# Norm statistics with tokens on partitions in a two-layer diffusion trunk

## The chip, the cores and the metric

The kernel is one program on one NeuronCore of a Trainium2 chip. The metric is the device time of one execution in microseconds (us). The engines are named as the profile names them: PE is TensorE's matmul, PEld its load of the stationary operand, DVE is VectorE, ACT is ScalarE, POOL is GpSimd, and SP issues the DMAs. They run side by side and meet at semaphores.

## The reference, cut to what matters

The trunk has two layers over 256 context tokens and 256 latent tokens, each with 1024 channels. A layer is a half-step SwiGLU, a token mixing of four head groups, and a second half-step SwiGLU. Every branch is normalised before it (with a modulation) and after it (with a gate):

```python
def rms_norm(x, g):
    y = xf * lax.rsqrt(jnp.mean(xf * xf, axis=-1, keepdims=True) + RMS_EPS)
    return y * g
def modulate(x, g_pre, shift, scale):
    return rms_norm(x, g_pre) * (1.0 + scale) + shift
def half_ffn(v, shift, scale, gate, g_pre, g_post, w1, w3, w2):
    out = swiglu(modulate(v, g_pre, shift, scale), w1, w3, w2)
    return v + 0.5 * gate * rms_norm(out, g_post)
```

These norms run over the 1024 channels of a token, so each needs one number per token: the reciprocal root of the mean of squares. There are twelve of them, six per layer. In the last layer the context tokens are dropped after the mixing, so three of the twelve cover the 256 latent tokens only.

## The kernel before, in words

The activations lie transposed in SBUF: channels on the 128 partitions, in `KC` = 8 blocks `m`, and the `T` = 512 tokens along the free dimension (four tiles of 128 tokens; tiles 0 and 1 are context, 2 and 3 latent). A sum over channels is thus a sum over partitions, done on PE, and the result has to be spread back over all partitions.

One norm has four steps. (1) `token_sums` (line 806): for each block of squares and each tile of 128 tokens one matmul with 32 columns of ones as the stationary operand and the 128 columns of squares as the moving one. Tile `i` writes partitions `32*i` to `32*i+31` of a PSUM bank, columns 0 to 127. (2) ACT `norm` (line 1535): a root over that [128 x 128] region into `root`. (3) DVE `norm` (line 2073): its reciprocal into `inverse`. (4) `spread` (line 796): one matmul per tile, a column of the constants that picks the tile's row (broadcast to 128 columns) as the stationary operand and `inverse` as the moving one, which puts the tile's 128 reciprocals on every partition of bank columns `128*i` and on. DVE then multiplies by the bank.

The twelve norms sit in these places. The first is at the start (`start_sums`, line 813; squares by DVE in `setup_x`), behind the products of the first modulation pieces. Ten more make five pairs, each pair in a gap between two long stages of weight products: `postnorm` (line 833) closes a branch, and `prenorm` (line 819) opens the next. The twelfth closes the last layer. In `postnorm` DVE has already added up seven of the eight blocks of squares into `yacc`, so that PE sums two blocks: `yacc` and the last one. Then DVE scales the eight blocks (line 2132) and adds them to `xT` (line 2136; two of the adds on POOL, line 2728). In `prenorm` ACT squares each block as soon as it is added (line 1573), and PE sums all eight blocks one after the other, in the order in which they come.

Each gap also has three products of the modulation (`mod_product`, line 786, 16 matmul records each), written into PE's order by hand: the first ahead of the postnorm's sums, the second behind the prenorm's sums of block `m == 2`, the third between the last sums and the `spread`. PE executes in program order. After the spread, DVE and ACT work through the eight blocks (DVE line 2100, ACT lines 1593 and 1599, DVE line 2109), and PE takes each block for the first weight piece of the next stage as it comes. The weights are split in two parts of lower precision by ACT (line 1533) and DVE (line 2024), and a weight product is three matmuls (lines 853 to 855). The DMAs of the weights wait for slots of a ring and not for the norms.

Of the kernel before, what the change touches and what calls it, by code (L numbers as in the profile page):

```python
# [20 lines left out]
ACT = mybir.ActivationFunctionType  # L21
AX = mybir.AxisListType.X

P = 128
# [12 lines left out]
C_TILE = C_SEL + 32  # L37
# [50 lines left out]
def trunk(nc, out, consts, x, c, ctx, c_ctx, w_mod, b_mod, norm_g, ffn1_w1, ffn1_w3, ffn1_w2,  # L88
# [3 lines left out]
    LAYERS, D, _ = w_in.shape  # L92
# [10 lines left out]
    NT = T // P  # L103
# [64 lines left out]
    MOD_GROUPS, at = [], 0  # L168
# [21 lines left out]
    with es:  # L190
        ARENA = 30336

        def sb(name, shape):
            return es.enter_context(nc.sbuf_tensor(name, shape, F32))
# [7 lines left out]
        cst = sb("cst", [P, C_END])  # L202
# [11 lines left out]
        epsc = sb("epsc", [P, 2])  # L214
# [10 lines left out]
        def sem(name):  # L225
            if name not in sems:
                sems[name] = es.enter_context(nc.semaphore(name))
            return sems[name]

        ident = cst[:, C_IDENT:C_IDENT + P]  # L230
        ones = cst[:, C_ONES:C_ONES + P]
# [5 lines left out]
        def view(at, *shape, parts=slice(0, P)):  # L237
            n = int(np.prod(shape))
            v = arena[parts, at:at + n]
            if len(shape) == 1:  # L240
                return v
            names = "abcd"[:len(shape)]
            return v.rearrange(f"p ({' '.join(names)}) -> p {' '.join(names)}",
                               **{k: s for k, s in zip(names, shape)})
# [14 lines left out]
        silu_t = view(27648, 2, T)  # L259
        sq_in, u_in = view(8192, KC, T), view(0, KC, T)  # L260
        ul_spare = view(7680, T)
        root, inverse = view(28160, P), view(28288, P)
        yacc = view(28672, T)

        convT = view(0, 12, T)
# [125 lines left out]
        inverse_ready, inverse_spread = sem("inverse_ready"), sem("inverse_spread")  # L391
# [9 lines left out]
        sums_ready, rms_ready = sem("sums_ready"), sem("rms_ready")  # L401
# [100 lines left out]
        def tiles_of(hs):  # L502
            return [2 * h + i for h in hs for i in range(2)]
# [22 lines left out]
        def quadrants(hs):  # L526
            return slice(64 * hs[0], P)
# [209 lines left out]
        def _(pe):  # L737
# [58 lines left out]
            def spread(n, bank, hs):  # L796

                pe.wait_ge(inverse_ready, n + 1)
                at = quadrants(hs)
                for i in tiles_of(hs):  # L800
                    last = pe.matmul(bank[:, i * P:(i + 1) * P],  # L801
                                     cst[at, C_TILE + i:C_TILE + i + 1].to_broadcast([P - at.start, P]),
                                     inverse[at, :], start=True, stop=True)
                last.then_inc(inverse_spread, 1)

            def token_sums(bank, squares, hs, first, last):

                for i in tiles_of(hs):
                    done = pe.matmul(bank[32 * i:32 * i + 32, 0:P], ones[:, 0:32], squares[:, i * P:(i + 1) * P],
                                     start=first, stop=last)  # L810
                return done

            def start_sums():
                for m in range(KC):
                    pe.wait_ge(x_squared, m + 1)
                    done = token_sums(ps[PRE_BANK], squares_of(0)[:, m, :], (0, 1), m == 0, m == KC - 1)
                done.then_inc(sums_ready, 1)

            def prenorm(l, j, second=None, third=None):
                hs = pre_halves(l, j)  # L820
                for m in range(KC):
                    pe.wait_ge(x_squared, 8 * (3 * l + j) + m + 1)
                    done = token_sums(ps[PRE_BANK], squares_of(j)[:, m, :], hs, m == 0, m == KC - 1)
                    if m == 2 and second is not None:
                        mod_product(second, ps[GAP_BANK])
                done.then_inc(sums_ready, 1)
                if third is not None:
                    mod_product(third, ps[GAP_BANK])
                spread(6 * l + 2 * j, ps[PRE_BANK], hs)
                if third is not None:  # L830
                    mod_turn(third, ps[GAP_BANK])

            def postnorm(l, j, first):
                hs = post_halves(l, j)
                q = 3 * l + j
                if first is not None:
                    mod_product(first, ps[GAP_BANK])
                pe.wait_ge(y_summed, (KC - 2) * (q + 1))
                token_sums(ps[POST_BANK], yacc, hs, True, False)
                pe.wait_ge(y_sq, KC * (q + 1))  # L840
                token_sums(ps[POST_BANK], ysq_of(j), hs, False, True).then_inc(sums_ready, 1)
                spread(6 * l + 2 * j + 1, ps[POST_BANK], hs)
# [615 lines left out]
            pe.wait_ge(sem("mod_params_in"), 16 * MOD_PARAM_DMAS)  # L1458
            setup_params(0, ps[2])
            spread(0, ps[PRE_BANK], (0, 1))  # L1460
            mod_group(2, ps[6])
            pe.wait_ge(mod_copied, 4)
# [19 lines left out]
        def _(act):  # L1482
            meet = meeting(act)
            link = linked(act, sem("act_link"))
            A = nc.scalar.activation
# [48 lines left out]

            def norm(n, bank, hs):
                act.wait_ge(sums_ready, n + 1)
                at = quadrants(hs)
                A(root[at, :], bank[at, 0:P], ACT.Sqrt, bias=epsc[at, 0:1], scale=1.0 / D).then_inc(rms_ready, 1)

            def gain(l, j, m, hs):  # L1540

# [24 lines left out]
            def prenorm(l, j, third=None):  # L1566

                hs = pre_halves(l, j)
                t0 = HALF * hs[0]
                p = 3 * l + j  # L1570
                for m in range(KC):
                    wait_x(act, p - 1, m)
                    A(squares_of(j)[:, m, t0:T], xT[:, m, t0:T], ACT.Square).then_inc(x_squared, 1)
                norm(6 * l + 2 * j, ps[PRE_BANK], hs)
                if third is not None:
                    mod_row_out(third, ps[GAP_BANK])
                prenorm_blocks(l, j, third)
# [25 lines left out]
            def gap(l, j):  # L1603
                third = gap_mods(l, j)[-1]
                hs = post_halves(l, j)
                norm(6 * l + 2 * j + 1, ps[POST_BANK], hs)
                for m in range(KC - 2, KC):
                    gain(l, j, m, hs)
                if after(l, j)[0] < LAYERS:
                    prenorm(*after(l, j), third)  # L1610
# [356 lines left out]
            mod_group(0, ps[0])  # L1967
            round_piece(PIECES["up0", 0, 0][0], 2048)
            norm(0, ps[PRE_BANK], (0, 1))
            setup_mod_params()  # L1970
            mod_group(2, ps[6])
# [19 lines left out]
        def _(dve):  # L1991
            meet = meeting(dve)
            link = linked(dve, sem("dve_link"))
            V = nc.vector
# [77 lines left out]

            def norm(n, hs):
                dve.wait_ge(rms_ready, n + 1)
                at = quadrants(hs)
                V.reciprocal(inverse[at, :], root[at, :]).then_inc(inverse_ready, 1)  # L2076

            def split_in(l, j):
                split_rest(PIECES["in", l][j], KC * IN_WIDTH[j], (wh_in, wl_in))
# [1 line left out]
            def prenorm(l, j):  # L2081
                hs = pre_halves(l, j)
                n = 6 * l + 2 * j
                pre_gains(l, j)
                norm(n, hs)
                prenorm_blocks(l, j)
# [36 lines left out]
            def postnorm(l, j, hs):  # L2123
                t0 = HALF * hs[0]
                q, n = 3 * l + j, 6 * l + 2 * j + 1
                norm(n, hs)
                dve.wait_ge(inverse_spread, n + 1)
                for m in range(KC + 1):
                    if m < KC:
                        y = uT[:, m, t0:T]  # L2130
                        dve.wait_ge(y_gained, KC * q + m + 1)
                        TT(y, y, ps[POST_BANK][:, t0:T], ALU.mult).then_inc(y_scaled, 1)  # L2132
                    if m and m - 1 not in POOL_ADDS:
                        dve.wait_ge(y_scaled, KC * q + m)
                        x = xT[:, m - 1, t0:T]
                        TT(x, x, uT[:, m - 1, t0:T], ALU.add).then_inc(x_ready, 1)  # L2136
# [539 lines left out]
            setup()  # L2676
            setup_x()
            norm(0, (0, 1))
            split_rest(PIECES["up0", 0, 0][0], 2048)
            dve.wait_ge(sem("params_act"), 1)  # L2680
# [231 lines left out]
```

## Time and profile before

| | us |
|---|---|
| median of 3 runs | 2231.27 |
| lowest and highest | 2228.21 and 2235.86 |
| the profiled execution, its own time | 2232.0 |
| span of the profiled execution | 2230.2 |
| PE busy in the span | 2080.8 (93%) |
| DVE, ACT, POOL busy | 1080.7, 795.0, 186.3 |

The span runs from the first to the last instruction, and 1.8 us of the execution's own time lie outside it. An fp32 matmul stands in the trace as two records, each with its own load record (PEld). A record's duration includes its way through the pipeline, so that neighbours overlap: what a stream of them costs is the distance from start to start. The column of the granted clock is a share of full speed: 1.00 is 2.4 GHz, 0.50 is 1.2 GHz.

### The profile page before, as it was taken

The numbers are of one execution on the slowest core, as the hardware profiler recorded it, in microseconds if no ns is written. First come the engines' busy times: TensorE is split into PE (matmuls) and PEld (weight loads), VectorE is DVE, ScalarE is ACT, GpSimd is POOL, SyncE is SP. The second block draws the span as 40 slices with busy tenths as digits, with TensorE's granted clock in tenths as the row PEclk, the third lists the DMA queues.
The fourth block names the chain that finished last, engine by engine and source line by source line (L and its number), as shares of the span: only waits on it lengthen the run. The fifth ranks groups of instructions, "written<-read, shape, count | busy, mean of one in ns | idle before, by whom it ended". The sixth has DMA issues, their size and how long they took to land.

```text
span 2230.2 us, 30926 instructions
## 1 busy us (share of the span) xinstructions
PE 2080.8 (93%) x13065; PEld 1711.7 (77%) x13065; DVE 1080.7 (48%) x1604; ACT 795.0 (36%) x1203; POOL 186.3 (8%) x288
## 2 busy tenths in 40 slices
PE   6999999899989998999999899999979987879997
PEld 4778888687846876888888688888858865678997
DVE  5233334566285586333334533333475557575555
ACT  4232223454336335222223522222253434245343
POOL 0000000100024321000000100000010023420000
PEclk9999999899999999999999999999988998999999
DMA  9563442422236424324323432432332311345662
GB/s 303 158 176 115 132 115 84 134 83 93 73 116 221 145 90 111 97 72 127 95 71 111 130 89 78 126 95 66 115 115 70 110 35 58 114 133 161 178 165 84
DMA packets 403322, 258.92 MB, mean 116 GB/s; under 512 B 21850, under 2 KB 402032, under 8 KB 403184
## 3 DMA queue, kind: packets, MB, share of 16 engines
q1 hardware_dynamic: 403184, 256.94, 39.3%
q8 instruction: 103, 1.69, 0.3%
q14 instruction: 35, 0.29, 0.0%
HBM read 255.86 MB, written 1.05 MB: 115 GB/s over the span
## 4 chain that ended last, share of the span: by engine, by line
PE 81%; DVE 12%; ACT 3%; issue 2%; SPq 1%; POOL 1%; DMA 0%; DVEq 0%; ACTq 0%; POOLq 0%
PE bank L853 23%; PE bank L855 23%; PE bank L854 23%; PE bank L786 2%; DVE uT L2132 1%; PE bank L1220 1%; DVE mlaw L2358 1%; DVE arena L2365 1%; DVE xT L2136 1%; DVE small L2386 1%; PE bank L1358 1%; DVE wl L2024 1%; PE bank L801 1%; ACT wh L1533 0%; DVE arena L2076 0%
## 5 line engine op out<-in xcount | busy, mean ns | idle before, releaser
L853 PE MATMUL bank<-uh,wh 128*128 128x512 f32 (+1 forms) x1504 | 548.7, 365 | 14.5 <-DVE ul L2109 6.7
L854 PE MATMUL bank<-ul,wh 128*128 128x512 f32 (+1 forms) x1504 | 546.0, 363 | 0.0
L855 PE MATMUL bank<-uh,wl 128*128 128x512 f32 (+1 forms) x1504 | 545.8, 363 | 0.0
L2024 DVE TENSOR_TENSOR wl<-ring,wh 128x2048 fp32r<-128x2048 f32 (+1 forms) x155 | 312.4, 2016 | 156.2 <-ACT wh L1533 155.3
L1533 ACT ACTIVATE wh<-ring 128x2048 fp32r<-128x2048 f32 (+1 forms) x158 | 267.1, 1691 | 310.5 <-PE bank L855 293.2
L853 PEld LDWEIGHTS bank<-uh,wh 128*128 128x128 f32 x1504 | 286.5, 190 | 64.7 <-issue 12.2
L855 PEld LDWEIGHTS bank<-uh,wl 128*128 128x128 f32 x1504 | 286.2, 190 | 43.9
L854 PEld LDWEIGHTS bank<-ul,wh 128*128 128x128 f32 x1504 | 286.6, 191 | 42.8
L853 PE MATMUL bank<-hh,wh 128*128 128x512 f32 (+1 forms) x704 | 255.5, 363 | 1.4 <-DVE wl L2024 1.4
L855 PE MATMUL bank<-hh,wl 128*128 128x512 f32 (+1 forms) x704 | 255.2, 362 | 0.0
L854 PE MATMUL bank<-hl,wh 128*128 128x512 f32 (+1 forms) x704 | 255.2, 362 | 0.0
L2154 DVE TENSOR_TENSOR arena<-arena,bank 128x512 f32<-128x512 f32 (+1 forms) x88 | 54.6, 621 | 370.8 <-PE bank L855 370.8
L1629 ACT ACTIVATE hh<-arena 128x512 fp32r<-128x512 f32 (+1 forms) x88 | 50.9, 579 | 412.3 <-DVE arena L2154 412.3
L853 PEld LDWEIGHTS bank<-hh,wh 128*128 128x128 f32 x704 | 132.9, 189 | 22.3 <-DVE wl L2024 1.7
L855 PEld LDWEIGHTS bank<-hh,wl 128*128 128x128 f32 x704 | 132.9, 189 | 20.7
L854 PEld LDWEIGHTS bank<-hl,wh 128*128 128x128 f32 x704 | 132.9, 189 | 20.5
L853 PE MATMUL bank<-uTh,wh_in 128*128 128x512 f32 (+2 forms) x320 | 126.3, 395 | 13.0 <-DVE ul_in L2109 7.4
L855 PE MATMUL bank<-uTh,wl_in 128*128 128x512 f32 (+2 forms) x320 | 122.6, 383 | 0.0
L854 PE MATMUL bank<-ul_in,wh_in 128*128 128x512 f32 (+2 forms) x320 | 122.5, 383 | 0.0
L1627 ACT ACTIVATE arena<-bank 128x512 f32<-128x512 f32 (+1 forms) x88 | 47.9, 544 | 160.9 <-PE bank L855 160.9
L1686 ACT ACTIVATE arena<-bank 128x512 f32<-128x512 f32 (+5 forms) x64 | 30.5, 479 | 177.1 <-PE bank L855 176.8
L853 PEld LDWEIGHTS bank<-uTh,wh_in 128*128 128x128 f32 (+1 forms) x320 | 63.7, 199 | 31.5 <-issue 8.5
(322 smaller groups left out, 2660.6 us busy)
## 6 DMA issues: line engine op xcount, KB each, us to landing
ring<-in_ffn_w_dram SPq DMA_DIRECT2D x176, 512.0 KB, 5.2
ring<-in_w_mod_dram SPq DMA_DIRECT2D x134, 512.0 KB, 4.5
ring<-in_ffn_w_dram SPq DMA_DIRECT2D x64, 384.0 KB, 3.4
ring<-in_ffn_w_dram SPq DMA_DIRECT2D x64, 320.0 KB, 4.1
ring<-in_w_in_dram SPq DMA_DIRECT2D x40, 512.0 KB, 4.5
ring<-in_w_out_dram SPq DMA_DIRECT2D x16, 512.0 KB, 4.5
arena<-in_w_mod_dram SPq DMA_DIRECT2D x10, 512.0 KB, 8.6
ring<-in_w_in_dram SPq DMA_DIRECT2D x4, 544.0 KB, 5.4
```

The lines of the kernel that those rows point to most:

```text
L786: product = pe.matmul(bank[at, 256:512], scT[:, own:own + 32], weights[:, k * 256:(k + 1) * 256], start=g == first and k < 4, stop=g == fi ...
L801: last = pe.matmul(bank[:, i * P:(i + 1) * P], cst[at, C_TILE + i:C_TILE + i + 1].to_broadcast([P - at.start, P]), inverse[at, :], start=T ...
L853: pe.matmul(bank, w_hi, x_hi, start=first, stop=False)
L854: pe.matmul(bank, w_hi, x_lo, start=False, stop=False)
L855: return pe.matmul(bank, w_lo, x_hi, start=False, stop=last)
L1220: last = pe.matmul(bank[:, h * P:(h + 1) * P], gates[:, 5, t, c0:c0 + 1].to_broadcast([P, P]), tri(d), start=False, stop=h == NH - 1, skip ...
L1533: A(high[:, SPLIT[n] % 2, 0:floats], ring[:, n % RING, 0:floats], ACT.Copy).then_inc(wh_ready, 1)
L1627: A(silu_t[:, j % 2, t0:T], ps[2 * (j % 2)][:, t0:T], ACT.Silu).then_inc(silu_done, 1)
L1629: A(hh[:, j, t0:T], silu_t[:, j % 2, t0:T], ACT.Copy).then_inc(hh_ready, 1)
L1686: A(dst, src, ACT.Copy, scale=scale).then_inc(proj_copied, 1)
L2024: TT(low[:, b, 0:floats], at, high[:, b, 0:floats].bitcast(F32), ALU.subtract).then_inc(wl_ready, 1)
L2154: TT(ht, ht, ps[2 * (j % 2) + 1][:, t0:T], ALU.mult).then_inc(gated, 1)
```

## The change

The sums turn round. Each [128 x 128] tile of squares becomes the stationary operand, loaded in full, and a single column of ones the moving one. Tile `i`'s sums land in column `i` of the bank, one token per partition. The root and the reciprocal then work on [128 x 4] in place of [128 x 128] (on [128 x 2] where only the latent tokens count, in place of [64 x 128]). The spread takes a column of `inverse`, broadcast to 128 columns, as the stationary operand and the identity as the moving one. The number of matmuls does not change in any step, and neither do the order of the work or the semaphores.

```diff
-        root, inverse = view(28160, P), view(28288, P)
+        root, inverse = view(28160, NT), view(28288, NT)
...
                 pe.wait_ge(inverse_ready, n + 1)
-                at = quadrants(hs)
                 for i in tiles_of(hs):
-                    last = pe.matmul(bank[:, i * P:(i + 1) * P],
-                                     cst[at, C_TILE + i:C_TILE + i + 1].to_broadcast([P - at.start, P]),
-                                     inverse[at, :], start=True, stop=True)
+                    last = pe.matmul(bank[:, i * P:(i + 1) * P], inverse[:, i:i + 1].to_broadcast([P, P]), ident,
+                                     start=True, stop=True)
...
             def token_sums(bank, squares, hs, first, last):
                 for i in tiles_of(hs):
-                    done = pe.matmul(bank[32 * i:32 * i + 32, 0:P], ones[:, 0:32], squares[:, i * P:(i + 1) * P],
-                                     start=first, stop=last)
+                    done = pe.matmul(bank[:, i:i + 1], squares[:, i * P:(i + 1) * P], ones[:, 0:1],
+                                     start=first and i == tiles_of(hs)[0], stop=last, skip_group_check=True)
...
                 act.wait_ge(sums_ready, n + 1)
-                at = quadrants(hs)
-                A(root[at, :], bank[at, 0:P], ACT.Sqrt, bias=epsc[at, 0:1], scale=1.0 / D).then_inc(rms_ready, 1)
+                at = slice(2 * hs[0], NT)
+                A(root[:, at], bank[:, at], ACT.Sqrt, bias=epsc[:, 0:1], scale=1.0 / D).then_inc(rms_ready, 1)
...
                 dve.wait_ge(rms_ready, n + 1)
-                at = quadrants(hs)
-                V.reciprocal(inverse[at, :], root[at, :]).then_inc(inverse_ready, 1)
+                at = slice(2 * hs[0], NT)
+                V.reciprocal(inverse[:, at], root[:, at]).then_inc(inverse_ready, 1)
```

## Rows read from the trace of the kernel before

**Rows 1.** The page: busy time by engine, then the chain of waits by line.
```profile
PE 2080.8 (93%) x13065; PEld 1711.7 (77%) x13065; DVE 1080.7 (48%) x1604; ACT 795.0 (36%) x1203; POOL 186.3 (8%) x288
...
PE bank L853 23%; PE bank L855 23%; PE bank L854 23%; PE bank L786 2%; DVE uT L2132 1%; PE bank L1220 1%; DVE mlaw L2358 1%; DVE arena L2365 1%; DVE xT L2136 1%; DVE small L2386 1%; PE bank L1358 1%; DVE wl L2024 1%; PE bank L801 1%; ACT wh L1533 0%; DVE arena L2076 0%
```

**Rows 2.** Chain of waits, first gap: start us, us, what.
```profile
419.03 0.47 PE bank L809 x8
...
419.52 0.38 ACT arena L1538
...
419.92 0.96 DVE arena L2076
...
431.92 0.47 PE bank L809 x8
...
433.82 1.17 PE bank L801 x8
...
449.96 2.30 DVE wl_in L2024
```

**Rows 3.** Timeline, first gap: start us, us, instructions [idle before].
```profile
418.34 0.40 PE L809 MATMUL bank<-arena,cst 128*32 128x128 f32 x8
...
426.98 1.29 ACT L1573 ACTIVATE arena<-xT 128x512 f32<-128x512 f32 x2 [0.51 <-POOL xT L2728]
...
427.66 0.65 PE L809 MATMUL bank<-arena,cst 128*32 128x128 f32 x8 [0.48 <-ACT arena L1573]
...
428.09 1.93 PE L786 MATMUL bank<-ring,scT 128*32 128x256 f32 x16
...
429.79 1.29 PE L809 MATMUL bank<-arena,cst 128*32 128x128 f32 x24
...
432.16 1.05 PE L786 MATMUL bank<-ring,scT 128*32 128x256 f32 x16
```

**Rows 4.** Timeline of PE and PEld, full loads with few moving columns.
```profile
1764.19 1.98 PEld L1002 LDWEIGHTS bank<-gates,cst 128*128 128x128 f32 x16
...
1766.09 0.97 PEld L1005 LDWEIGHTS bank<-gates,cst 128*128 128x128 f32 x8
...
1766.12 1.04 PE L1005 MATMUL bank<-gates,cst 128*128 128x16 f32 x8
...
562.94 0.53 PEld L1005 LDWEIGHTS bank<-gates,cst 128*128 128x128 f32 x3
...
563.05 0.42 PEld L1005 LDWEIGHTS bank<-gates,cst 128*128 128x128 f32 x2
```

**Rows 5.** Lines L1939 (a root) and L2394 (a reciprocal): ns min/median/max.
```profile
L1939 ACT ACTIVATE std<-small,epsc x3: 281/281/283, 795.5 to 1971.1; 128x4 f32<-128x4 f32 x3
...
L2394 DVE RECIPROCAL small<-small x24: 138/156/167, 642.3 to 1878.6; 128x2 f32<-128x2 f32 x24
```

**Rows 6.** Windows: length, busy us (records) by engine, granted clock, DMA share, GB/s.
```profile
428.00:430.00 2.00, 2.00 (x28) 1.06 (x24) 2.00 (x5) 0.93 (x3) 1.66 (x1) 0.50 1.07 346
430.00:432.00 2.00, 1.47 (x39) 0.66 (x32) 1.54 (x5) 1.83 (x3) 0.00 (x0) 0.99 1.07 326
...
560.70:562.40 1.70, 1.70 (x17) 1.69 (x16) 0.00 (x0) 1.47 (x3) 0.00 (x0) 1.00 0.00 0
562.40:563.40 1.00, 1.00 (x10) 1.00 (x10) 0.00 (x0) 1.00 (x3) 0.00 (x0) 0.89 0.00 0
563.40:565.00 1.60, 1.60 (x5) 1.31 (x6) 0.77 (x5) 1.60 (x2) 0.00 (x0) 0.50 0.00 0
```

**Rows 7.** Timeline of PE, the start.
```profile
19.31 1.52 PE L809 MATMUL bank<-arena,cst 128*32 128x128 f32 x48
...
24.40 2.08 PE L801 MATMUL bank<-arena,cst 128*128 128x128 f32 x8 [1.61 <-DVE arena L2076]
```

**Rows 8.** Timeline of ACT, the start.
```profile
23.01 0.35 ACT L1538 ACTIVATE arena<-bank,epsc 128x128 f32<-128x128 f32 x1
...
34.69 0.38 ACT L1507 ACTIVATE mod_row<-bank 128x256 f32<-128x256 f32 x1 [0.38 <-PE bank L786]
```

**Rows 9.** Timeline, fifth gap, latent tokens only.
```profile
2007.72 1.71 PE L809 MATMUL bank<-arena,cst 128*32 128x128 f32 x14
...
2010.11 0.36 ACT L1538 ACTIVATE arena<-bank,epsc 64x128 f32<-64x128 f32 x1 [2.17 <-PE bank L809]
...
2011.51 0.71 PE L801 MATMUL bank<-arena,cst 64*128 64x128 f32 x4 [0.34 <-DVE arena L2076]
```

**Rows 10.** Chain of waits, the last norm.
```profile
2213.97 0.44 PE bank L809 x4
...
2214.43 0.37 ACT arena L1538
2214.83 0.96 DVE arena L2076
```

## The prediction

> **What bounds the kernel now.** I read the page first. PE is busy 93% of the span, and the chain that ended last runs through the three lines of weight products for 69% [rows 1]. The root (L1538), the reciprocal (L2076) and the spread (L801) stand in it with about 1% or less each. So the change can touch only the start, the five gaps and the last norm. The chain through the first gap comes next [rows 2]: the sums of the last block, root, reciprocal and spread follow each other with nothing beside them, in the postnorm (419.03 to 422.1) and in the prenorm (431.92 to 435.0). The chain then runs through DVE and ACT to the split of the next weights at 449.96. What the spread gains or loses, the end of the gap gains or loses. The timeline of the same gap [rows 3] shows how PE's own queue stands around that chain, and this decides the case. Four of the five gaps have all 512 tokens and look alike to within 0.1 us; the fifth and the last norm have 256.
>
> **The price of a sum.** Before, eight records (four tiles, two records each) cost little, because the load has 32 columns and the four tiles write four groups of partitions: 24 records, three blocks, take 1.29 us [rows 3], 0.05 us from start to start. Afterwards each record loads 128 columns. The nearest rows are the gate sums, full fp32 loads with 8 or 16 moving columns: sixteen loads in 1.98 us, then eight in 0.97 [rows 4]; less the 0.19 of one load, that is 0.11 us from start to start. At half clock the starts are 562.94 and 563.05 [rows 4], again 0.11. No row has a single moving column; 8 and 16 columns give the same, so I take 0.11 at either clock. A block of four tiles then costs 0.88 us on PE. The ends for one record are 0.05 (this kernel's 32-column records) and 0.13 (full loads with 128 columns in the spread: 1.17 us for eight, less the tail, at full clock).
>
> **Root and reciprocal.** The root now takes 0.37 us on [128 x 128]; a root on [128 x 4] takes 0.28 [rows 5]. The reciprocal takes 0.95; on [128 x 2] it takes 0.16 [rows 5]. Together they save 0.9 us a norm, bounded by 0.8 and 1.0.
>
> **Spread.** It has the same number of records, the same 128 loaded and 128 moving columns, and a broadcast stationary operand as before: nothing, at the same clock. With 256 tokens it now contracts over 128 rows and not 64; I take nothing there too, bounded by 0.1 either way.
>
> **Postnorm, 512 tokens (four).** The last sums stand in the chain with 0.47 us [rows 2]; eight full loads take 1.04 [rows 4], so +0.6. The sums of `yacc` start at 418.34 [rows 3] and ran beside DVE's square, which ends just before 419.03. At 0.11 us a record they now end about 0.1 later than that, so +0.1. With the 0.9 saved, each postnorm gains 0.2 us.
>
> **Prenorm, 512 tokens (four).** Here PE has a queue. Square 2 is ready at 427.6, its sums run at 427.66, the second product runs from 428.09 to 429.79, a start-to-start time of 1.70 us at half clock, and then three waiting blocks are caught up in 1.3 us, so that the last block is summed 0.5 us after its square, at 432.4 [rows 2, 3]. Afterwards, all moved 0.2 earlier by the postnorm: sums of block 2 end at 427.4 + 0.9 = 428.3; the product ends at 430.0; blocks 3 to 7 are forty records, 4.4 us, and end at 434.4. The squares no longer matter, they come every 0.6 us and a block costs 0.88. That is 2 us late. The root and the reciprocal follow (0.2 of PE's tail, 0.28, 0.16, the hops): ready at 435.1. But the third product stands ahead of the spread in PE's order. Before, it ran at 432.16 for 1.05 us [rows 3] under the root and the reciprocal, which were longer. Now it starts at 434.4 and ends at 435.4 at full clock, or at 436.1 if it takes 1.70 as the second one does at half clock. So the short root and reciprocal are worth nothing beyond this product, and the spread starts at 435.4 to 436.1 where it started at 433.82 [rows 2]: +1.6 to +2.3, the postnorm's gain already in it.
>
> **The clock.** Under the second product the granted clock was 0.50 (1.2 GHz), and it rose behind it, so that the third product and the spread ran at 2.4 GHz [rows 6]. Under the gate sums, full loads with 8 and 16 moving columns, PE was busy all the time; the clock was 1.00 in their first part, 0.89 in the second, and 0.50 behind them, though PE had not been idle [rows 6]. The new sums are such work, with one column. So 4.4 us of them between the second product and the spread can leave the spread at 1.2 GHz. There it costs 2.08 us [rows 7] and not 1.17: +0.9 a gap. I take about half of this: one full gap costs 1.6 (warm throughout) to 3.2 us (cold throughout), taken at 2.4. Four make +9.6, bounded by 6.4 and 12.8. The Trainium skill, "TensorE: Matmul & The Clock Gate" (Part 1), says that the gate follows how busy PE has been; by that rule alone the new sums would hold the clock up, and the sum would be the warm one. The row of the gate sums disagrees.
>
> **Start.** The sums start at 19.31 behind the modulation products [rows 7]; 64 records at 0.11 take 7 us and end at 26.3. The root started at 23.01 [rows 8]: +3.3, less 0.9, so the spread starts 2.4 later than 24.40, and it ran at half clock already [rows 7]. Behind it PE's modulation products and ACT's blocks move by as much. At 34.69 ACT had waited 0.38 us for a product behind a DMA [rows 8]; this absorbs a part, a clock that rises earlier another. I take +1.8, bounded by 1.2 and 2.4.
>
> **256 tokens.** The fifth gap's sums run at half clock, 14 records in 1.71 us, already 0.1 a record [rows 9], so they do not grow. The root waits for PE as before at 2010.11, and the third product now ends beside the old start of the spread at 2011.51: −0.3. Its postnorm and the last norm have four records: 0.44 [rows 10] becomes about 0.65, and 0.9 goes: −0.7 each. Together −1.7, bounded by −2.2 and −1.
>
> **Sum.** 9.6 + 1.8 − 1.7 = +9.7 us on the profiled execution's own 2232.0 us: 2241.7. That execution lies 0.7 us above the median of the runs; against the median I predict 2241 us, 0.4% slower. All parts at their warm ends give 6.4 + 1.2 − 2.2 = +5.4, at their cold ends 12.8 + 2.4 − 1.0 = +14.2, so the forecast's own range is 2237 to 2246. What a measurement of this kernel tells from no change is 0.3%, 6.7 us.
>
> **Rivals.**
>
> *The loads turn out cheap (faster).* If a full load hides behind its predecessor, a record costs what the old ones cost. Then root and reciprocal pay: −1.0 in each postnorm; in each prenorm the third product ends at 433.2 and lets the spread start 0.6 earlier. Four gaps give −6.4, the fifth and the last −2.4, the start nothing, since ACT's root there waited for ACT itself: 2222. It decides below 0.07 us a record: 428.3 + 1.7 + 40 records + 1.0 then meets 433.82. For it: weight products with 512 columns hide their loads. Against it: 0.11 us in 24 rows of the gate sums [rows 4]. The same page (back-to-back issue gap) gives about 60 cycles for a matmul with 1 to 64 columns, 25 ns, when the load is left out; by that rule this rival would be the forecast.
>
> *Warm and absorbed (no change).* The clock stays at 2.4 GHz in the gaps, the second product too (0.7 us less in each), and the start is absorbed: 4 × 1.0 + 1 − 1.7 = +3.3, 2234 to 2238. For it: the clock rises in the gap today, with sums among the work (0.99 in the stretch behind the second product) [rows 6]. Against it: before that product DVE and ACT leave PE idle in every gap, and the clock is at 0.50 there now [rows 6].
>
> *The cold clock reaches into the next stage (slower still).* If it also delays the weight products behind the spread by more than PE's idle time at the end of the gap (the wait for the split at 449.96 [rows 2]), each gap costs 2 us more: +20, 2248 to 2253. Against it: these products follow DVE's and ACT's pace.
>
> **Chances.** Forecast 0.52, no change 0.25, cold beyond 0.13, faster 0.10. The forecast's lowest part lies within 0.3%. This makes faster 0.10, same 0.31, slower 0.59. The range takes in the no-change case from 2233 up and the cold one to 2251.
>
> **What would show it.** After: PEld records of L809's line with 128 columns, 0.11 us apart; a root near 0.28 and a reciprocal near 0.16; in the four full gaps the last prenorm sums end 2 us later behind an unbroken row of loads, the third product directly behind, the spread directly behind that, not behind the reciprocal; the spread at 2.1 us in some gaps; the last norm 0.7 shorter. Records 0.06 apart, or PE waiting for squares again, would make it wrong.

## The result, and the profile after

| | before | after |
|---|---|---|
| median, us | 2229.95 (4 runs, 2228.21 to 2235.86) | 2278.98 (4 runs, 2276.77 to 2283.06) |
| ratio to before | 1 | 1.0205, 95% interval [1.0174, 1.0236] |
| the profiled execution: own time, span, mean granted clock | 2232.0, 2230.2, 0.968 | 2283.06, 2281.3, 0.947 |

The change makes the kernel 2% slower, 49 us, where 10 us were predicted. The profiled execution after is the longest of its four and lies 4 us above their median. The clock has two levels, so a mean of 0.947 over 2281.3 us means 2 × 0.053 × 2281.3 = 242 us at half clock; before it was 2 × 0.032 × 2230.2 = 143 us.

The page of the kernel after: busy time by engine, the granted clock in 40 slices, the chain by line, and the groups of the sums' line.

```profile
PE 2152.7 (94%) x13065; PEld 1789.0 (78%) x13065; DVE 1072.1 (47%) x1604; ACT 794.1 (35%) x1203; POOL 186.2 (8%) x288
...
PEclk8999999799999997999999799999979998898998
...
PE bank L851 23%; PE bank L853 22%; PE bank L852 22%; PE bank L807 4%; PE bank L786 3%; PE bank L1218 1%; PE bank L800 1%; DVE mlaw L2356 1%; PE bank L1356 1%; DVE arena L2363 1%; PE bank L1121 1%; DVE wl L2022 1%; ACT uT L1591 1%; DVE small L2384 1%; PE bank L1327 0%
...
L807 PEld LDWEIGHTS bank<-cst,arena 128*128 128x128 f32 x432 | 82.9, 297 | 22.4 <-ACT arena L1571 17.7
L807 PE MATMUL bank<-cst,arena 128*128 128x1 f32 x432 | 84.4, 328 | 14.9 <-ACT arena L1571 13.3
```

PE is busier than before (94% against 93% of a longer span) and does no more products: as many records, 13065, as in [rows 1]. The sums (L807 now, L809 before) have entered the chain with 4%, some 90 us; the reciprocal has left its list. The first gap shows how. Chain of waits of the kernel after: start us, us, what.

```profile
424.14 1.89 PE bank L807 x16
426.06 0.27 ACT arena L1536
...
426.59 1.17 PE bank L800 x8
...
430.26 0.64 ACT arena L1571
430.95 5.28 PE bank L807 x24
436.23 1.86 PE bank L786 x16
438.09 8.62 PE bank L807 x40
446.71 1.86 PE bank L786 x16
448.57 2.02 PE bank L800 x8
...
463.57 1.91 ACT wh_in L1531
465.56 2.30 DVE wl_in L2022
```

From 430.95 to 450.6 everything is PE. Before, the chain went through squares, root and reciprocal here [rows 2, 3]. The forty records after the second product take 8.62 us, 0.215 each. The sixteen of the postnorm take 1.89, 0.118 each with the tail of the last one; their load records alone take 1.86 us, which less the 0.19 of one load is 0.11 from start to start. The same instruction has two prices, and the windows of the kernel after say what goes with them (length, busy us of PE, PEld, DVE, ACT and POOL with their records, granted clock, DMA share, GB/s):

```profile
424.00:426.00 2.00, 2.00 (x20) 1.86 (x16) 0.60 (x1) 1.09 (x1) 0.83 (x1) 1.00 0.00 0
427.00:431.00 4.00, 0.80 (x8) 0.61 (x6) 3.22 (x5) 1.55 (x4) 2.77 (x2) 0.66 0.07 7
431.00:435.00 4.00, 4.00 (x19) 4.00 (x20) 4.00 (x8) 2.43 (x4) 2.65 (x2) 0.50 1.01 328
...
438.02:446.64 8.62, 8.62 (x44) 8.61 (x41) 0.00 (x0) 0.00 (x0) 0.00 (x0) 0.50 0.42 129
...
451.00:458.00 7.00, 4.70 (x13) 3.67 (x13) 6.39 (x12) 6.30 (x13) 0.00 (x0) 0.50 0.40 116
458.00:463.00 5.00, 5.00 (x22) 4.08 (x21) 4.25 (x8) 4.53 (x8) 0.00 (x0) 0.90 0.00 0
```

PE is idle between the postnorm's spread and the first square of the prenorm, and the clock falls there (a mean of 0.66 from 427 to 431). In the kernel before it was at 0.50 under the second product, too, and up again behind it [rows 6]. Now it stays at 0.50 through 8.62 us in which PE is busy without a gap, through the third product and the spread, and on into the weight products until about 458.

The line of the sums, of the root and of the reciprocal (ns min/median/max) in the kernel after:

```profile
L807 PEld LDWEIGHTS bank<-cst,arena x432: 186/333/338, 19.1 to 2266.1; 128*128 128x128 f32 x144
...
L1536 ACT ACTIVATE arena<-bank,epsc x12: 262/263/264, 30.4 to 2266.4; 128x4 f32<-128x4 f32 x9, 128x2 f32<-128x2 f32 x3
...
L2074 DVE RECIPROCAL arena<-arena x12: 165/178/179, 30.6 to 2266.7; 128x4 f32<-128x4 f32 x9, 128x2 f32<-128x2 f32 x3
```

The root (0.26) and the reciprocal (0.18) are as short as they were priced. A load is 186 ns at its shortest and 333 in the median, so more than half of the 432 loads ran at the low clock.

Where the 51.1 us of span went. Each row is a stretch of the two traces. A gap is taken here from the start of the postnorm's spread to the start of the split of the next weights on DVE (L2024 before, L2022 after).

| stretch | before | after | difference |
|---|---|---|---|
| start to the first postnorm's spread | 420.9 | 426.6 | +5.7 |
| four full gaps | 29.0, 28.4, 28.4, 29.0 | 39.0, 39.1, 38.2, 38.6 | +40.0 |
| from each to the next postnorm's spread | 407.0, 354.2, 354.2, 350.8 | 409.9, 354.2, 354.3, 350.6 | +2.8 |
| fifth gap | 20.2 | 24.8 | +4.6 |
| from there to the end | 208.0 | 206.0 | −2.0 |

So the loss is in the gaps and at the start. Behind the spread nothing is added but the spread's own length: in the first gap it ends at 434.99 before and at 450.59 after, and the split follows 14.97 us behind both; the other three are alike. The weight products at half clock until 458 are not on the chain. In the long stages the two kernels are level, but for 2.9 us in the first layer's token mixing. No experiment separates these; e10 below, with the same start and prenorms, does not have them.

### The profile page after: what moved, and what is told of

The parts are those of the page before. It is cut to its first block, busy times and chain, and to the rows that moved or that the text cites. A ratio compares the mean times of both kernels' runs of the same rounds, so it can differ in the third digit from the quotient of the medians.

```text
span 2281.3 us, 30926 instructions
## 1 busy us (share of the span) xinstructions
PE 2152.7 (94%) x13065; PEld 1789.0 (78%) x13065; DVE 1072.1 (47%) x1604; ACT 794.1 (35%) x1203; POOL 186.2 (8%) x288
## 4 chain that ended last, share of the span: by engine, by line
PE 84%; DVE 10%; ACT 3%; issue 1%; POOL 1%; DMA 0%; DVEq 0%; SPq 0%; ACTq 0%; POOLq 0%
PE bank L851 23%; PE bank L853 22%; PE bank L852 22%; PE bank L807 4%; PE bank L786 3%; PE bank L1218 1%; PE bank L800 1%; DVE mlaw L2356 1%; PE bank L1356 1%; DVE arena L2363 1%; PE bank L1121 1%; DVE wl L2022 1%; ACT uT L1591 1%; DVE small L2384 1%; PE bank L1327 0%
## 5 line engine op out<-in xcount | busy, mean ns | idle before, releaser
L2022 DVE TENSOR_TENSOR wl<-ring,wh 128x2048 fp32r<-128x2048 f32 (+1 forms) x155 | 312.5, 2016 | 152.1 <-ACT wh L1531 151.3
L807 PEld LDWEIGHTS bank<-cst,arena 128*128 128x128 f32 x432 | 82.9, 297 | 22.4 <-ACT arena L1571 17.7
L807 PE MATMUL bank<-cst,arena 128*128 128x1 f32 x432 | 84.4, 328 | 14.9 <-ACT arena L1571 13.3
```

Of the source, the lines that this page charges most:

```text
L807: done = pe.matmul(bank[:, i:i + 1], squares[:, i * P:(i + 1) * P], ones[:, 0:1], start=first and i == tiles_of(hs)[0], stop=last, skip_gr ...
L2022: TT(low[:, b, 0:floats], at, high[:, b, 0:floats].bitcast(F32), ALU.subtract).then_inc(wl_ready, 1)
```

## The experiments

The theory for all of them: the sums lose by what they do on PE, in the prenorms and at the start, and half of the loss is the clock. Such loads with one moving column cost 0.11 us at 2.4 GHz and 0.215 at 1.2 GHz, and they do not bring the clock back. The rival: something in the order of the work (third product ahead of the spread, short root and reciprocal with nothing to hide) costs it, and the clock is a bystander.

**e1: 128 moving columns.** The ones become 128 columns, and the root reads one column of each tile; all else is as in the kernel after.

```diff
-                    done = pe.matmul(bank[:, i:i + 1], squares[:, i * P:(i + 1) * P], ones[:, 0:1],
+                    done = pe.matmul(bank[:, i * P:(i + 1) * P], squares[:, i * P:(i + 1) * P], ones,
```

> The changed kernel, but each full load of squares is followed by 128 moving columns of ones and not by one (the same sums in 128 columns, the root reads one of them). Same number of loads and records. Theory A (one moving column leaves PE's clock at 1.2 GHz behind the first idle stretch of a gap, and a full load takes twice as long there): 128 moving columns let the clock rise in the gap, the time at half clock falls from 244 us to 150-190, and the kernel takes 2240-2258 us, faster than the changed one (2279) although it does more. Theory B (PE's time for full loads alone, the clock follows how long PE is busy): no gain, 2279-2290 us, time at half clock still about 240.

Measured: 2246.18 us, ratio 1.0052 [1.0036, 1.0067]. Three quarters of the loss (2.05% in the kernel after, 0.52% here) is gone by adding work. The time at half clock is 126 us, less than the 150 to 190 expected. Chain and then windows of this kernel, first gap:

```profile
424.78 5.49 PE bank L807 x24
430.27 1.20 PE bank L786 x16
431.46 4.66 PE bank L807 x40
436.13 1.00 PE bank L786 x16
437.13 1.10 PE bank L800 x8
```

```profile
424.78:430.20 5.42, 5.42 (x25) 5.20 (x25) 5.42 (x10) 3.26 (x6) 3.28 (x2) 0.50 1.03 334
430.20:431.40 1.20, 1.20 (x18) 0.46 (x17) 0.80 (x4) 1.12 (x2) 0.00 (x0) 0.81 0.77 237
431.40:436.10 4.70, 4.70 (x48) 4.58 (x47) 0.00 (x0) 0.00 (x0) 0.00 (x0) 1.00 0.75 232
```

At 0.50 a record takes 0.229 us, hardly more than with one column; then the clock rises during the second product, and the forty records take 0.117 each. So the moving columns hardly change the pace at either clock, and the price of a load doubles, nearly, when the clock halves. With one moving column the clock did not come back here, with 128 it did.

In the third gap of this kernel the clock is never down. Windows, and the postnorm's spread and the split of the next weights from the chain:

```profile
1248.00:1255.80 7.80, 5.12 (x47) 3.90 (x46) 6.99 (x12) 4.09 (x8) 3.08 (x2) 1.00 0.57 144
1255.80:1262.00 6.20, 6.20 (x64) 5.45 (x61) 2.02 (x7) 2.48 (x5) 0.25 (x1) 1.00 0.62 169
```

```profile
1247.62 1.17 PE bank L800 x8
...
1277.58 2.30 DVE wl L2022
```

From spread to split it is 30.0 us, where this gap takes 28.4 before and 38.2 after. So with every load at full clock the queue on PE costs 1.6 us in this gap, and the other 8.2 of the change's 9.8 go with the low clock. The other three full gaps of e1, whose first 24 loads run at half clock as above, cost 3.6 to 4.0 us. These and the start make up what is left, 0.52% or some 12 us.

**e2: the long root and reciprocal back.** On top of the former, ACT and DVE work on 128 columns again (and the spread picks its columns of `inverse` accordingly).

```diff
-                A(root[:, at], bank.rearrange("p (i n) -> p i n", n=P)[:, at, 0], ACT.Sqrt, bias=epsc[:, 0:1], scale=1.0 / D).then_inc(rms_ready, 1)
+                A(root.rearrange("p (i n) -> p i n", n=32)[:, at, :], bank.rearrange("p (i n) -> p i n", n=P)[:, at, 0:32], ACT.Sqrt, bias=epsc[:, 0:1], scale=1.0 / D).then_inc(rms_ready, 1)
...
-                V.reciprocal(inverse[:, at], root[:, at]).then_inc(inverse_ready, 1)
+                V.reciprocal(inverse[:, 64 * hs[0]:P], root[:, 64 * hs[0]:P]).then_inc(inverse_ready, 1)
```

> As e1_wide, with the long root and reciprocal of before (128 columns of [128 x 128]) put back; the sums' form is that of e1_wide. It prices what the change gains. Theory A: six postnorms stand on the chain and lose 0.9 us each (0.26 to 0.37 and 0.18 to 0.95), the prenorms nothing, because the third product stands ahead of the spread: e1_wide + 5 us (4 to 7). Rival: root and reciprocal are on the chain in all twelve norms: + 10 us.

Measured: 2252.41 us, 1.0086 [1.0066, 1.0106], 6.2 us above the former. So the short forms are worth about 6 us over twelve norms, 0.5 each and not the 0.9 that they save on their engines. That fits the expectation that the rest hides behind the third product. A part of the 6 us may be the clock, whose mean is 0.970 here and 0.972 in e1.

**e3 and e4: warming PE, after and before.** Three fp32 matmuls with 512 moving columns, whose result nobody reads, go into PE's idle time between the postnorm's spread and the prenorm's first sum; once in the kernel after, once in the kernel before.

```diff
+            def warm(n):
+                for _ in range(n):
+                    pe.matmul(ps[1][:, :], ones, cst[:, 0:512], start=True, stop=True)
...
                 if after(l, j)[0] < LAYERS:
+                    warm(3)
                     prenorm(*after(l, j), second, third)
```

> The changed kernel with three extra matmuls (ones by 512 constant columns, fp32, result unused) in PE's idle time between the postnorm's spread and the prenorm's first sums, about 2.6 us of work at 2.4 GHz. Theory A (it is the one-column sums that hold the clock down): the clock stays up for the first blocks and falls during the long row of sums all the same; 2262-2276 us. Theory C (the idle time ahead of the sums puts the clock down and the sums would hold a clock that is up): full clock through the gap, 2238-2250 us.

> The kernel before with the same three extra matmuls in each gap. Theory A: the second product runs at 2.4 GHz and not at 1.2, but the sums there wait for ACT's squares anyway, so 0 to 0.5 us a gap: 2227-2231 us. Rival: the extra matmuls stand in front of the first sums and push the queue: 2231-2236 us.

Measured: after 2268.29 us, 1.0147 [1.0121, 1.0173]; before 2233.71, 1.0003 [0.9992, 1.0014]. Windows of the warmed kernel after, first gap:

```profile
431.00:433.90 2.90, 2.90 (x29) 2.70 (x31) 2.90 (x6) 1.79 (x4) 1.56 (x2) 0.99 1.07 364
433.90:436.00 2.10, 2.10 (x19) 0.83 (x18) 2.10 (x4) 1.57 (x3) 1.00 (x1) 0.50 1.09 352
436.00:440.00 4.00, 4.00 (x20) 4.00 (x21) 0.49 (x4) 0.82 (x2) 0.00 (x0) 0.50 0.88 240
```

This is the clearest look at the sums. The 24 records of blocks 0 to 2 run at 0.99. Behind them the clock is at 0.50, under the second product and under the forty records, though PE was not idle for a moment. In the third gap it falls within the first 24 records, in the second and fourth within the forty (at 0.50 from 889.0 and from 1669.0). Only in the fifth, with 12 and then 20 records in 4.7 us, it stays at 1.00. So such sums do not hold the clock in the full gaps; the gate sums had shown a fall like it [rows 6]. The warming brings 11 us and leaves most of the forty records in each gap slow.

The kernel before gains nothing by it, and 2233.71 lies above the 2227 to 2231 expected, in the range of the rival; against 2232.65, the median of the kernel before in the same comparison, there is no difference. Its first gap now stands at 1.00 from 425 to 436, and the stretch from the postnorm's root to the prenorm's is 12.9 us as before. The low clock was not what the gap waited for.

**e5: squares in rounded fp32.** Squares of the start and of the prenorms are written in the rounded type of the weight products. A sum is then one record and not two, so four records a block.

```diff
+                    done = pe.matmul(bank[:, 2 * i:2 * i + 2], squares[:, i * P:(i + 1) * P], ones_r[:, :],
...
-            return sq_in if j == 1 else sq
+            return sq_in_r if j == 1 else sq_r
```

> The changed kernel with the squares of the prenorms and of the start written in the rounded fp32 type that the weight products use, so that a block's sums are four records and not eight (two moving columns, the least this form took). Theory A: the clock stays low as in the changed kernel, but a block costs 4 x 0.215 = 0.86 us at half clock and not 1.72; the last sums of a full prenorm come 4 us earlier, the start 5 us: 2279 - 24 = 2255 us (2248-2262), time at half clock about 200 us. Rival (the number of loads is not what the row of sums costs): within 6 us of 2279.

Measured: 2244.79 us, 1.0047 [1.0031, 1.0063], a smaller loss than expected, and outside the range. A record is still 0.218 us (twenty in 4.36), the clock still low. But a block is now 0.87 us at half clock, so that the sums of blocks 0 to 2 keep up with their squares; in the kernel after these 24 records alone took 5.28. The number of loads counts, as the theory says.

**e6: rounded, 128 moving columns.** Both at once; from e1 I expected the clock to rise.

```diff
-                    done = pe.matmul(bank[:, 2 * i:2 * i + 2], squares[:, i * P:(i + 1) * P], ones_r[:, :],
+                    done = pe.matmul(bank[:, i * P:(i + 1) * P], squares[:, i * P:(i + 1) * P], ones_r[:, :].unsqueeze(1).to_broadcast([P, 2, N_ONES]),
```

> e5_round with 128 moving columns of ones behind each load. Theory A: both halves of the cost go, the queue in front of the prenorm's spread (half the loads) and the half clock (columns): 2229-2237 us, level with the kernel before. Rival (something else of the change costs, the spread's new operands or the one-column results): it stays above 2242 us.

Measured: 2246.77 us, 1.0066 [1.0047, 1.0085]. A miss. Window of its twenty records behind the second product, first gap:

```profile
431.23:435.70 4.47, 4.47 (x26) 4.35 (x22) 0.97 (x5) 1.27 (x3) 0.00 (x0) 0.50 0.97 301
```

128 columns of the rounded type leave the clock at 0.50. "Enough moving columns" was too simple a theory. The time falls in the rival's range, but what the rival names is not it: e9 below has the spread's new operands and one-column results in six norms and loses nothing.

**e7: the third product behind the spread**, on top of e1. ACT reads that product later, too, behind the first block; the diff shows PE's part.

```diff
-                if third is not None:
-                    mod_product(third, ps[GAP_BANK])
                 spread(6 * l + 2 * j, ps[PRE_BANK], hs)
                 if third is not None:
+                    mod_product(third, ps[GAP_BANK])
```

> e1_wide with the third product of each gap moved behind the spread (ACT reads it after the first block instead of before it). It tests the step that says the third product stands between the sums and the spread: at full clock it takes 1.0 us, the root and the reciprocal 0.5 us, so 0.5 us a gap come back, five gaps: e1_wide - 2.5 us (1 to 4), about 2243 us. Rival: what follows on ACT and PE takes it back, no difference from e1_wide (2246) or slower.

Measured: 2244.4 us, 1.005 [1.0033, 1.0067]. 1.8 us less than e1, but the intervals lie over each other: the order is worth little or nothing that can be told. The rival that blames it falls where the clock is up. In the kernel after, where the third product takes 1.86 us ahead of the spread, moving it was not run.

**e8: all twelve norms rounded, 128 columns, third product behind the spread**: e6 with the edit of e7, and the squares and `yacc` of the postnorms rounded too. It was meant as the best version.

```diff
-                token_sums(ps[POST_BANK], yacc, hs, True, False)
+                rounded_sums(ps[POST_BANK], yacc_r, hs, True, False)
```

> All cures together: rounded squares and 128 moving columns in every norm, the third product behind the spread. Theory A: each postnorm keeps 0.8 us (root and reciprocal 0.88 shorter, sums level), each prenorm has its spread 0.9 us earlier: 6 x 0.8 + 5 x 0.9 = 9 us under the kernel before: 2223 us (2218-2228). Rival: level with the kernel before, 2230-2235.

Measured: 2240.94 us (11 runs), 1.004 [1.0029, 1.0051]. Missed too, and for the reason of e6, since it was priced at full clock. Its window 430 to 436:

```profile
430.00:436.00 6.00, 6.00 (x37) 4.61 (x36) 3.44 (x9) 2.67 (x5) 1.66 (x1) 0.50 1.01 310
```

**e9 and e10: postnorms only, prenorms only.** The kernel before with the new form in the six postnorms, and the kernel after with the old form in them.

```diff
-                token_sums(ps[POST_BANK], yacc, hs, True, False)
+                column_sums(ps[POST_BANK], yacc, hs, True, False)
```

```diff
-                    done = token_sums(ps[PRE_BANK], squares_of(j)[:, m, :], hs, m == 0, m == KC - 1)
+                    done = column_sums(ps[PRE_BANK], squares_of(j)[:, m, :], hs, m == 0, m == KC - 1)
```

> One half of the change: the six postnorms take the new form in full (one moving column, fp32), the start and the five prenorms keep the old one. Theory A: a postnorm is 16 loads at full clock, behind PE's long stage; its sums cost 0.6-0.7 us more and root and reciprocal 0.9 less, four times -0.2, twice -0.7: -2 us, 2228-2233, no difference that can be measured; the clock in the gaps as before. Rival (the form itself spoils the gap wherever it stands, by the clock it leaves behind): 2240 us or more.

> The other half: the start and the five prenorms in the new form, the six postnorms in the old one. Theory A: all of the loss is here, 2275-2285 us, time at half clock about 240 us. Rival: the loss splits between both halves, 2250-2268.

Measured: postnorms only 2231.32 us (11 runs), 0.9995 [0.9984, 1.0005]; start and prenorms only 2278.66, 1.0199 [1.0184, 1.0214]. The whole loss is in the start and the prenorms. In a postnorm the sums follow weight products, the clock is at 1.00, there are two blocks and not eight, and what the loads cost, root and reciprocal give back. (In the fifth postnorm of the kernel after it falls, to a mean of 0.78 under the last sums and 0.50 under the spread.)

**e11: postnorms only, with their squares rounded.** Since a postnorm's loads run at the full clock, halving their number should turn it into a gain.

```diff
-                token_sums(ps[POST_BANK], yacc, hs, True, False)
+                column_sums(ps[POST_BANK], yacc_r, hs, True, False)
```

> e9_post_only with the postnorm's two blocks of squares written in the rounded fp32 type, so that its sums are four records a block (two moving columns). From the last square to the spread the kernel before took 1.93 us and e8_best 1.28, so 0.6 us in each of six postnorms: 2232 - 4 = 2228 us (2225-2231). Rival: nothing, since the gap behind it changes its clock: 2231-2236.

Measured: 2227.93 us (12 runs, 2222.52 to 2239.85), 0.9978 [0.9964, 0.9992]. It is the one version that beats both kernels, by 0.2%, less than the 0.3% that one measurement of three runs can tell; the interval of the twelve runs excludes 1 all the same. Its chain, first gap:

```profile
419.77 1.12 PE bank L821 x8
420.92 0.27 ACT arena L1551
421.21 0.19 DVE arena L2095
421.45 1.17 PE bank L804 x8
```

From the end of the first product (419.77) to the spread it is 1.68 us; with sixteen fp32 records, in the kernel after, it is 2.45 (424.14 to 426.59).

**e12: every rounded sum twice.** What separates e1 (clock rises) from e6 (stays low) is the type and the number of records. Here e6 issues each sum twice, the copy into a bank that nobody reads, so that it has the eight loads of 128 moving columns a block that e1 has.

```diff
+                    pe.matmul(ps[1][:, i * P:(i + 1) * P], squares[:, i * P:(i + 1) * P],
+                              ones_r[:, :].unsqueeze(1).to_broadcast([P, 2, N_ONES]), start=True, stop=True)
```

> The kernel e6_round_wide (squares of start and prenorms in rounded fp32, 128 moving columns) with every sum issued twice, the second into a bank that nobody reads: 8 load records a block instead of 4, as many as the fp32 form has. Theory A, what raised the clock in e1_wide is the number of load-and-stream records in one uninterrupted stretch, whatever their type: the clock rises inside the doubled sums as in e1_wide, and the kernel comes out near e1_wide, 2246 us (2241 to 2250). Theory B, it is the type (fp32 records against rounded ones): the sums stay at clock 0.50 and the doubled ones add 32 records of 0.217 us, about 7 us, at each of the four full gaps and the start, so 2246.8 + 30 = about 2277 us (2268 to 2285).

Measured: 2274.12 us, 1.0195 [1.0178, 1.0212], as expected by the theory of the type. Window of its forty records behind the second product:

```profile
432.80:441.40 8.60, 8.60 (x42) 8.48 (x42) 0.00 (x0) 0.00 (x0) 0.00 (x0) 0.50 0.42 130
```

This row is almost the one of the kernel after (438.02 to 446.64), with 128 columns in place of one; e1, with fp32 records of the same shape and count, was at 1.00 in this place. So the number of records is not what raised the clock in e1. The type is left, and one difference beside it: e6 and e12 read the moving ones as 64 columns twice over, e1 as 128 columns where they lie. These two were not taken apart, and why either should count, no run here shows.

## Why the prediction was wrong

The direction and the place were right. The size was wrong by a factor of five (49 for 9.7), and the time lies far outside the range of 2233 to 2251.

**The price of a sum: the step that failed.** "I take 0.11 at either clock." At full clock that holds: 0.11 from start to start. At half clock it is 0.215. The two starts at 562.94 and 563.05 [rows 4] were no starts at half clock. The window that holds them has a mean of 0.89 [rows 6], and from 562.90 to 563.10 alone the granted clock is 1.00; it fell just behind. One pair of starts was too little for "at either clock". And a row that says otherwise was among those shown: eight records with full loads at the start, at half clock, take 2.08 us [rows 7], and 1.17 at full clock [rows 2].

**The clock: too timid.** I read from the gate sums that such loads do not hold the clock, and then let it fall for the spread alone, by half. In fact the gap begins low and nothing in it brings the clock up. Step by step in the first gap, counted from the postnorm's spread, which starts 5.66 us later than before: the second product begins another 2.5 later (the prediction has 0.4), since the 24 records ahead of it take 5.28; the product takes 1.86 and not 1.70 [rows 3]; from its end to the root it is 8.7 us and not 2.6; from the root to the spread 0.4 more, since the third product takes 1.86; the spread itself takes 2.02 and not 1.17. Together that is the +9.9 of the table, where the prediction has 2.4. In the four gaps it makes 30 us of the 39 missed. The largest part is the forty records, 8.62 where I had 4.4: 17 us in four gaps.

**Prenorm: mechanism right.** An unbroken row of loads, the third product directly behind, the spread directly behind that and not behind the reciprocal: all three stand in the chain. And where the clock is at 1.00 throughout, in the third gap of e1, the gap costs 1.6 us, which is what the prediction has for "warm throughout" (its 1.6 has the postnorm's 0.2 taken off, the measured one has not). (That the four full gaps "look alike to within 0.1 us" was misread: from root to root they take 12.9, 12.3, 12.3 and 12.9. Nothing hangs on it.)

**Root and reciprocal: right.** 0.26 and 0.18 where 0.28 and 0.16 were taken; and, as predicted, "worth nothing beyond this product" for a part (e2).

**Postnorm: right within the noise, a little too good.** −0.2 each was predicted. In the first gap the spread stands 3.37 us behind the end of the weight products (DVE L2173, 417.56 to 420.93) before and 3.41 after (L2171, 423.18 to 426.59), so the two sides are level; the sixteen loads ended 0.2 later than I had them. e9 is within its uncertainty of no change. **Last norm: right.** −0.7 predicted; from DVE's scaling behind the last weight product to the spread it is 2.80 us before and 2.10 after.

**Fifth gap: wrong**, for the reason of the first step: −0.3 predicted for the start of its prenorm's spread, +4.6 measured from the postnorm's spread to the split. "Already 0.1 a record" was the 32-column record at half clock; the full load takes twice that there, twenty in 4.36 us.

**Start: wrong.** +1.8 predicted, +5.6 measured at the first weight product. The kernel before, then the kernel after:

```profile
35.60 0.48 PE L853 MATMUL bank<-uh,wh 128*128 128x512 f32 x1
```

```profile
41.20 0.47 PE L851 MATMUL bank<-uh,wh 128*128 128x512 f32 x1
```

The 64 records take 11.15 us and not 7, since the clock is low for a part of them too (a mean of 0.63 from 19 to 31 us). The root came at 30.35, 7.3 later than before; the short root and reciprocal gave 0.9 of it back, and another 0.9 was absorbed behind the spread. So the absorption was there, and the sums' price was wrong.

**The rivals.** The cold clock that reaches into the next stage did not happen, though it is the nearest to the measured time. Its condition was that the weight products behind the spread come late by more than PE's idle time. The clock was low behind the spread until about 458, but the split of the next weights keeps its distance of 14.97 us to the spread's end, and two of the four stages behind are level to within 0.1 us. The loss lies ahead of the spread, in the sums. "Loads cheap" falls with 0.11 a record at full clock, "warm and absorbed" with the windows. By the rule of the Trainium skill that the prediction weighed, "TensorE: Matmul & The Clock Gate" (Part 1), by which the gate follows how busy PE has been, the sums would hold the clock. The window 438.02 to 446.64, 8.62 us busy of 8.62 at 0.50, and e3's fall from 0.99 to 0.50 in the midst of busy PE disagree, if the profile's busy time is what is meant.

## What to carry to other kernels

A matmul with a full load and one moving column is priced by its load, and the load by the clock: count 0.11 to 0.12 us at 2.4 GHz and 0.22 at 1.2 GHz, and ask first at which clock the place is. In the full gaps here a long run of such loads did not keep PE's clock and did not bring it back, so in a gap where the clock is low all that stands behind them is slow too; put them behind dense products and keep them few, as in the postnorms here. A duration that is to hold at both clocks needs rows from well inside a stretch of each, not from its edge.

## What the runs showed of the hardware

- A load of 128 columns: 0.11 to 0.12 us from start to start at 2.4 GHz (one column, the kernel after; 128 columns, e1), 0.215 to 0.229 at 1.2 GHz, whether one (the kernel after), two (e5) or 128 columns (e1, e6) move.
- PE busy without a gap for 8.6 us at a granted clock of 0.50 (kernel after, and e12), and a fall from 0.99 to 0.50 behind such sums without any idle time (e3). Not every such row ends in a fall: in e3's fifth gap the clock stays at 1.00, and the 24 gate sums, with 0.50 behind them in the kernel before [rows 6], have 1.00 under and behind them in the kernel after (576 to 582).
- With fp32 records of 128 moving columns the clock came back within the gap (e1); with as many rounded fp32 records of 128 moving columns it did not (e6, e12). Whether the type or the way in which the ones are read counts is open.
- A low clock by itself need not cost: the kernel before has 143 us at half clock, and warming its gaps (e4: 116 us) changes nothing that can be measured.
